# Decode trunk on one core: VectorE's sample steps moved ahead of its projection work, the mLSTM gate exponents in two row halves, the last norm's spread on ScalarE

## The chip, the cores and the metric

One core of a Trainium2 chip. The metric is the device time of one execution in microseconds (us); 3 runs of the kernel before have a median of 925.68 us, from 924.83 to 926.03.

## The reference, cut to what matters

One layer of a decoder over 512 prompt tokens and 32 sample tokens (8 sequences of 4, each with 2048 past positions in a paged cache), all in float32.

```python
z = x @ w_in + b_in                               # 27 feature tiles of 128
qk = silu(causal_dwconv(m_qk, width 4))           # mLSTM queries and keys
h = mlstm_chunkwise(q, k, v, ig, log_sigmoid(f))  # weights exp(b_t - b_s + i_s - m_t), causal
o_c, o_s, o_w = nsa_attend(...)                   # compressed, top-16 selected, window keys
mix = [sigmoid(o) * head_norm(h), g0*o_c + g1*o_s + g2*o_w]
x1 = layer_norm(ALPHA*x + mix @ w_out)
y  = layer_norm(ALPHA*x1 + (gelu(conv(u_a)) * conv(u_b)) @ w_down)   # u = x1 @ w_up
```

For the samples, attention over the past needs the keys of 16 pages of each of the 8 sequences transposed, scored, and the values of the same pages read once more. The mLSTM weights of a chunk come as one exponent per pair of tokens: the input gate less the running sum of the forget gates of one token, less the running maximum of the other.

## The kernel before, in words

Features stand on partitions, the 544 tokens on columns. The large products (projection, output, up, down) are made of tiles: the function `project` (L1867) runs 8 steps of k, each with 6 matmuls (a weight split in a high and a low part, against high and low parts of the input, each on 256 and on 288 columns). ScalarE makes the high part of a weight piece (`split_hi`, L500, which waits until the tile two before has ended), VectorE the low part (`split_lo`, L508), each two tiles ahead. A tile writes one of two PSUM pairs, so tile n+2 waits (`evicted`, L2100) until the result of tile n has been taken out: by VectorE (`rows_out`) for tiles 1 to 10 and 23 to 26, by ScalarE for the gates (0), the eight mLSTM query and key tiles 11 to 18 (`conv_rows`, followed by VectorE's `rows_conv`, L1148, four operations of 568 columns) and the sigmoid tiles 19 to 22 (`sigmoid_rows`, L808).

The samples' attention is woven into the projection tiles 5 to 26. Its order is written out by hand: `decode_halves` (L138) yields halves (g, i, h), with g the group of four sequences, i the beat (four of window keys from -4, then one for each four pages of a quad), h the half of a beat; `halves_of_tiles` (L188) gives each a tile and the step k of that tile after which TensorE runs it. Tiles 5 to 20 take five halves each, after steps 0, 2, 3, 5 and 7; tiles 21 to 26 take four, after 0, 2, 4 and 6. TensorE transposes keys, scores them, compresses them, and for the group before transposes probabilities and sums values. A half belongs to all engines. ScalarE runs the copies, exponentials and so on of the halves of tile n+1 in its turn n: the first of them right behind `split_hi`, then tile n's own result, the second, `silu`, and then the others. VectorE runs the halves of tile n in its turn n, all of them before `split_lo` of tile n+2 and before the results of tile n (L1367), so behind the results of tile n-1. Its steps: the eviction of scores (`past_scores`, L1268), the selection of the 16 best blocks (`select`, L1299), the probabilities of the selection (`selected_probs`, L1317) and of the window (`window_probs`, L1263). Transposed keys and probabilities and scores share PSUM banks 5 and 6 in turn (`next_bank`, L1896): a bank is free when what it held two turns before has been taken out.

Pages come by DMA into a ring of 8 slots. Two queues issue them: SP the even pages of a beat, POOL the odd ones (`stream_keys` and `stream_values`, L540 and L572). Both take the halves in order; a key page of beat i+2 waits for the slot that TensorE frees in beat i. SP's queue carries the weights too. POOL, behind its last issue, sets up the mLSTM exponents.

Then comes a stage of prompt attention (32 pairs of scores, softmax, transposes, values) with the four mLSTM chunks woven in. In each chunk TensorE makes the gate exponents (`exponents`, L2251) as a product over 40 rows: `gl` (L237) holds the gate differences in rows 0 to 7 and ones in rows 32 to 39, `rows` (L297) holds a unit pattern against the first and the negated running maxima against the second (POOL, `masked_rows`, L724). Two matmuls of 512 columns, one for each half of the heads, write banks 2 and 3; VectorE takes them out in `decay` (L1451). The output, up and down products follow. The last norm ends the kernel: token sums on TensorE, variance on VectorE, root on ScalarE, reciprocal and a diagonal matrix on VectorE (`inverse`, L1738), a product with ones that spreads it (`spread`, L2412), multiplication out of PSUM on VectorE, scale and bias on ScalarE (L1127), and the store.

Of the kernel before, what the change touches and what calls it, by code (L numbers as in the profile page):

```python
# [18 lines left out]
ALU = mybir.AluOpType  # L19
# [168 lines left out]
def halves_of_tiles():  # L188

    body = [x for x in decode_halves() if x[0] < GROUPS]  # L190
    tail = [x for x in decode_halves() if x[0] >= GROUPS]
    out = [[] for _ in range(ZT)]
    for n, x in enumerate(body):
        t = len(body) // (TAIL - FIRST)
        out[FIRST + n // t].append(((0, 2, 3, 5, 7)[n % t], x))
    for n, x in enumerate(tail):
        out[TAIL + n // 4].append(((0, 2, 4, 6)[n % 4], x))
    return out


# [3 lines left out]
def layer(nc, a):  # L204
    with ExitStack() as ctx:
# [28 lines left out]
        gfx = sb("gfx", [64, NT])  # L234
        gf = gfx[0:8, :]
        dsc = sb("dsc", [128, 1256])
        gl = sb("gl", [40, NT])  # L237
        gi = gl[0:8, :]
        ga = sb("ga", [8, NT])
        gmx = sb("gmx", [40, T])  # L240
# [53 lines left out]
        comb = smem[:, 3072:3592].rearrange("p (q t e) -> p q t e", q=2, t=4)  # L294
        sq = smem[:, 3592:4104].rearrange("p (h d) -> p h d", h=H)
        carried = zt[:, Z_G, 0:520].rearrange("p (s t e) -> p s t e", s=2, t=4)
        rows = mixt[0:40, 0:4, :].rearrange("p k c -> p (k c)")[:, 0:2048].rearrange("p (s c) -> p s c", s=2)  # L297
        hc = zt[:, Z_MV:Z_MV + 4, :].rearrange("p k c -> p (k c)")[:, 0:2048].rearrange("p (j h d) -> p j h d", j=4, h=H)
        wv = zt[:, Z_SV:Z_CV + 1, :].rearrange("p k c -> p (k c)")[:, 0:2080].rearrange("p (i h c) -> p i h c", i=4, h=H)

# [396 lines left out]
        @block.gpsimd  # L697
        def _(pool):

            pool.memset(uq[:, :, 0:3], 0.0).then_inc(prep, 1)  # L700
            pool.memset(ga[:, 0:T], 1.0).then_inc(prep, 1)
            pool.memset(gl[:, :], 0.0).then_inc(gl_set, 1)
            pool.wait_ge(gl_set, 1)
            pool.memset(gl[32:40, :], 1.0).then_inc(gl_set, 1)
            pool.wait_ge(gl_set, 2)
            pool.memset(qb, 0.0).then_inc(nd_z, 1)
            issued = [0]
            pool.wait_ge(xin[KD // 2 - 1], 16)
            for i in range(-SG, 0):
                stream_keys(pool, mybir.EngineType.Pool, 1, 0, i)  # L710
                issued[0] += 1
            pool.wait_ge(consts, NCONST)
            for n in range(ZT):
                for _, (g, i, h) in HALVES[n]:
                    stream(pool, mybir.EngineType.Pool, 1, issued, g, i, h)
            pool.wait_ge(nd_s, SETS * GROUPS)
            pool.memset(rows, 0.0).then_inc(gl_set, 1)
            pool.wait_ge(gl_set, 3)
            for s in range(2):
                pool.tensor_copy(by_block(rows[0:8, s]).rearrange("p (q t) c -> p q t c", q=2),  # L720
                                 bc(by_head(ident[0:8, 0:8]), 128)).then_inc(ml_rc, 1)
            pool.wait_ge(ml_rc, 2)

            def masked_rows(c):  # L724
                if c >= 2:
                    pool.wait_ge(ml_d, c - 1)
                    pool.wait_ge(ml_wv, c + 1)
                pool.tensor_tensor(by_block(rows[32:40, c % 2]).rearrange("p (q t) c -> p q t c", q=2),
                                   gm_neg[:, 128 * c:128 * c + 128].unsqueeze(1).unsqueeze(1).broadcast_to([8, 2, 4, 128]),
                                   bc(by_head(ident[32:40, 32:40]), 128), ALU.mult).then_inc(ml_r, 1)  # L730
                pool.wait_ge(ml_r, c + 1)

            for c in range(2):
                masked_rows(c)
            pool.wait_ge(w_used, ZT)
            pool.memset(tv[:, :, :, HD:HD + 1], 1.0).then_inc(prep, 1)
            pool.memset(scp, 0.0).then_inc(np_z, 1)
            pool.wait_ge(g_em, 1)
            pool.wait_ge(prep, 3)
            pool.wait_ge(tok_k_ev, 2 * (QT + 1))  # L740
            pool.wait_ge(stored, 16 * 3)
            for i in range(QT):
                pool.wait_ge(tok_v_ev, i + 1)
                pool.tensor_tensor(wv[:, i, :, :], tv[:, i, :, :], bc(emp[:, 64 + 8 * i:72 + 8 * i], HD + 1),
                                   ALU.mult).then_inc(ml_wv, 1)
                if i >= 2:
                    masked_rows(i)

            pool.wait_ge(np_pv, PAIRS)
            pool.memset(qm, 0.0).then_inc(sd_qz, 1)  # L750

            pool.wait_ge(sd_sc, 2)
            pool.wait_ge(sd_in, 48)
            pool.wait_ge(sd_int, 2)
            for t in range(4):
                c3 = ctv[:, t, :].rearrange("p (b e) -> p b e", b=NB)
                pool.tensor_tensor(c3, c3, bc(scb[:, 8 * t:8 * t + 8], HD), ALU.mult).then_inc(sd_cm, 1)
            pool.wait_ge(sd_end, 2)
            pool.wait_ge(hist, 16)
            pool.memset(uf[:, :, 0:2], 0.0).then_inc(prep, 1)  # L760
            for n in range(UP):
                pool.wait_ge(f_u, n + 1)
                pool.tensor_copy(fc[:, n, 0:2], uf[:, n % 4, 512:514])  # L763
                pool.tensor_copy(fc[:, n, 2:18].rearrange("p (b t) -> p b t", b=NB),
                                 by_sequence(uf, n, 6)[:, :, 4:6]).then_inc(f_last, 1)

        @block.scalar
        def _(act):
# [353 lines left out]
            act.activation(mean[:, T:NT], q4[2][:, 1, HALF:HALF + NS], ACT.Copy).then_inc(ln_act, 1)  # L1122
            act.activation(s4[:, 0:1], epsc[:, :], ACT.Sqrt)
            root(1)
            for m in range(KD):
                act.wait_ge(ln_u, m + 1)
                act.activation(xt[:, m, :], xt[:, m, :], ACT.Identity, bias=vec("ln2_b", m),  # L1127
                               scale=vec("ln2_w", m)).then_inc(ln_y, 1)

        @block.vector  # L1130
        def _(dve):
# [232 lines left out]
                    to_mix(p - 1)  # L1364

            for n in range(ZT):
                for _, half in HALVES[n]:  # L1367
                    decode_half(*half)
                if n == 4:
                    rows_out(n)  # L1370
# [14 lines left out]
                    table_rows()  # L1385
                if n == 3:
                    gate_columns()

            def token_columns(i):
                dve.wait_ge(tok_t, 3 * i + 1)  # L1390
# [347 lines left out]
            def inverse(n):  # L1738

                dve.wait_ge(ln_act, act_stat(n, "root"))  # L1740
                link(dve.reciprocal(tok5[:, :], tok5[:, :]))
                dg = scaled[0]
                dve.tensor_tensor(by_block(dg[:, 0:T]), ident.unsqueeze(1).broadcast_to([128, 4, 128]),
# [113 lines left out]
            for m in range(3, KD):  # L1857
                last = centred(m)
            link(last)
            dve.wait_ge(ln_pe, pe_stat(1, "spread"))  # L1860
            for m in range(KD):
                dve.tensor_tensor(xt[:, m, 0:T], xt[:, m, 0:T], bank[6], ALU.mult)
                dve.tensor_tensor(xt[:, m, T:NT], xt[:, m, T:NT], bank[7][:, 0:NS], ALU.mult).then_inc(ln_u, 1)

        @block.tensor
        def _(pe):
# [384 lines left out]
            def exponents(c):  # L2251
# [5 lines left out]
                    pe.wait_ge(tok_v_ev, QT + 1)  # L2257
                    pe.wait_ge(tok_k_ev, 2 * QT + 2)
                for q in range(2):
                    mm = pe.matmul(bank[2 + q], gl[:, token_rows(c)], rows[:, c % 2, 512 * q:512 * q + 512],  # L2260
                                   start=True, stop=True)
                mm.then_inc(ml_d, 1)

            def states(c):
# [145 lines left out]
                token_means(norm_rows[0][2], bank[7]).then_inc(ln_pe, 1)  # L2410

            def spread(n):  # L2412
                pe.wait_ge(ln_dve, 2 * n + 2)
                pe.matmul(bank[6], ones, scaled[0][:, 0:T], start=True, stop=True)
                pe.matmul(bank[7][:, 0:NS], ones, scaled[0][:, T:NT], start=True, stop=True).then_inc(ln_pe, 1)

# [172 lines left out]
```

## Time and profile before

| | us |
|---|---|
| median of 3 runs | 925.68 |
| profiled execution, its own time | 931.38 |
| its span, first to last instruction | 929.4 |
| TensorE busy | 865.3 (93%) |
| VectorE busy | 594.2 (64%) |
| ScalarE busy | 406.0 (44%) |
| GpSimd busy | 134.6 (14%) |
| mean granted TensorE clock | 0.938 of full |

All times of rows are from the start of the span. Busy times of TensorE are of pipelined matmuls: an engine that is 100% busy at a granted clock of 0.50 does half the work. Projection with the samples' attention lies at 0 to 289 us, prompt attention with the mLSTM at 289 to 440, output and up products to about 780, down and the last norm behind it.

### The profile page before, as it was taken

To read this page: it belongs to the slowest core of one execution; us is meant where nothing else is said; L and a number is where in the kernel's file an instruction comes from. 1 tells how busy PE (TensorE), PEld (TensorE's weight loads), DVE (VectorE), ACT (ScalarE), POOL (GpSimd) and SP (SyncE) were. 2 spreads that over 40 slices of the span, in tenths; PEclk is the share of its full clock that TensorE was granted. 3 is DMA by queue.
4 is the path that set the end of the run, shared out by engine and by line. 5 is a ranking of instruction groups with operands and counts; after the bars stand their busy time and mean duration, and the time that the engine had idled before them with its cause. 6 is when DMAs were issued, how large, how long until landed. Compare 5 with 4: busy or idle time off the path is not lost.

```text
span 929.4 us, 20070 instructions
## 1 busy us (share of the span) xinstructions
PE 865.3 (93%) x7843; PEld 784.5 (84%) x7843; DVE 594.2 (64%) x1227; ACT 406.0 (44%) x769; POOL 134.6 (14%) x248
## 2 busy tenths in 40 slices
PE   6999989898988899897889999999999999999994
PEld 6998878777877666665769999999999999999993
DVE  4622336541433687877887678888888888755556
ACT  4332345543523233477233355655555556222213
POOL 2022213253432200000010011111111111000000
PEclk9999989899989577999689999999999999999997
DMA  9267686677566000000214245222222222223212
GB/s 325 71 214 241 228 282 216 211 229 229 154 213 227 2 1 1 1 1 8 98 47 130 89 159 181 92 92 81 80 92 91 92 85 73 91 80 94 87 58 96
DMA packets 54888, 112.46 MB, mean 121 GB/s; under 512 B 7089, under 2 KB 32466, under 8 KB 54282
## 3 DMA queue, kind: packets, MB, share of 16 engines
q1 hardware_dynamic: 47074, 90.54, 29.7%
q0 software_dynamic: 6528, 17.83, 6.2%
q10 hardware_dynamic: 1192, 2.81, 0.8%
q8 instruction: 62, 1.02, 0.4%
q14 instruction: 32, 0.26, 0.1%
HBM read 105.54 MB, written 12.40 MB: 127 GB/s over the span
## 4 chain that ended last, share of the span: by engine, by line
PE 80%; DVE 10%; issue 4%; DMA 2%; ACT 2%; POOLq 2%; POOL 0%; ACTq 0%; SPq 0%; DVEq 0%
PE q L1883 32%; PE q L1881 29%; PE q L2204 2%; PE q L2220 2%; PE q L2230 2%; PE q L1945 1%; POOLq L517 1%; DVE xt L1428 1%; PE q L1933 1%; DMA arena<-in_pool 1%; PE q L2294 1%; DVE xt L1441 1%; PE q L1999 1%; PE q L1956 1%; PE q L2194 1%
## 5 line engine op out<-in xcount | busy, mean ns | idle before, releaser
L498 DVE TENSOR_TENSOR wring_r<-wring,whi_r 128x1024 fp32r<-128x1024 f32 (+1 forms) x101 | 120.2, 1191 | 162.3 <-ACT whi_r L495 162.0
L1881 PE MATMUL q<-arena_r,whi_r 128*128 128x256 f32 x712 | 212.4, 298 | 11.9 <-DVE wring_r L498 8.9
L1883 PE MATMUL q<-arena_r,whi_r 128*128 128x288 f32 (+1 forms) x712 | 214.1, 301 | 0.0
L1883 PE MATMUL q<-arena_r,wring_r 128*128 128x288 f32 (+1 forms) x712 | 213.7, 300 | 0.0
L1881 PE MATMUL q<-arena_r,wring_r 128*128 128x256 f32 x712 | 202.8, 285 | 0.0
L495 ACT ACTIVATE whi_r<-wring 128x1024 fp32r<-128x1024 f32 (+1 forms) x101 | 104.4, 1035 | 212.9 <-PE q L1883 212.5
L1883 PE MATMUL q<-xt_r,whi_r 128*128 128x290 f32 (+1 forms) x552 | 166.1, 301 | 0.0
L1881 PEld LDWEIGHTS q<-arena_r,whi_r 128*128 128x128 f32 x712 | 137.4, 193 | 23.4 <-DVE wring_r L498 8.9
L1881 PE MATMUL q<-xt_r,whi_r 128*128 128x256 f32 x552 | 157.0, 284 | 0.0
L1881 PEld LDWEIGHTS q<-arena_r,wring_r 128*128 128x128 f32 x712 | 137.5, 193 | 0.0
L1883 PEld LDWEIGHTS q<-arena_r,whi_r 128*128 128x128 f32 x712 | 137.5, 193 | 0.1
L1883 PEld LDWEIGHTS q<-arena_r,wring_r 128*128 128x128 f32 x712 | 137.2, 193 | 0.0
L1881 PEld LDWEIGHTS q<-xt_r,whi_r 128*128 128x128 f32 x552 | 106.4, 193 | 0.0
L1883 PEld LDWEIGHTS q<-xt_r,whi_r 128*128 128x128 f32 x552 | 106.1, 192 | 0.0
L987 ACT ACTIVATE whi<-q 128x128 f32<-128x128 f32 (+3 forms) x64 | 24.9, 436 | 67.3 <-PE q L2230 67.2
L553 POOL DMA_DIRECT2D arena<-in_pool x64 | 34.7, 542 | 132.3 <-PE q L1945 66.1
L826 ACT ACTIVATE mixt<-q 128x512 f32<-128x512 f32 x40 | 23.9, 598 | 68.0 <-PE q L1933 56.9
L1883 PE MATMUL q<-zt_r,whi_r 128*128 128x288 f32 x176 | 51.9, 297 | 0.0
L1881 PE MATMUL q<-zt_r,whi_r 128*128 128x256 f32 x176 | 49.0, 280 | 0.0
L763 POOL COPY smem<-zt 128x2 f32<-128x2 f32 x42 | 8.8, 211 | 247.1 <-ACT zt L1097 247.1
L581 POOL DMA_DIRECT2D arena<-in_pool x64 | 34.4, 537 | 53.8 <-issue 25.1
L1096 ACT ACTIVATE zt<-cst,sm 128x512 f32<-128x512 f32 x42 | 30.5, 727 | 26.5 <-DVE cst L1800 26.5
(458 smaller groups left out, 1564.0 us busy)
## 6 DMA issues: line engine op xcount, KB each, us to landing
wring<-in_w_up SPq DMA_DIRECT2D x42, 512.0 KB, 3.4
wring<-in_w_in SPq DMA_DIRECT2D x27, 512.0 KB, 5.0
arena<-in_pool SPq DMA_DIRECT2D x64, 192.0 KB, 3.5
arena<-in_pool POOLq DMA_DIRECT2D x64, 192.0 KB, 4.3
wring<-in_w_down SPq DMA_DIRECT2D x24, 448.0 KB, 3.2
arena<-in_pool SPq DMA_DIRECT2D x64, 64.0 KB, 2.2
arena<-in_pool POOLq DMA_DIRECT2D x64, 64.0 KB, 2.6
wring<-in_w_out SPq DMA_DIRECT2D x8, 512.0 KB, 7.1
```

Of the source, the lines that this page charges most:

```text
L495: return eng.activation(out, src, ACT.Copy)
L498: return eng.tensor_tensor(out, src, hi.bitcast(F32), ALU.subtract)
L553: eng.dma_start(pages[:, o % PAGE_RING, :], rows[k][:, 0:384]).then_inc(pg_land[o % PAGE_RING], 16)
L581: eng.dma_start(home[:, s, :], rows[s][:, 384:512]).then_inc(land, 16)
L826: act.activation(skt[i % SG], t, ACT.Copy).then_inc(nd_te, 1)
L987: act.activation(ptb[:, m % 2, g, 0:w], bank[4 + g][:, 0:w], ACT.Copy).then_inc(np_te, 1)
L1096: act.activation(u[:, 2:514], t[:, 0:T], ACT.Identity, bias=b, scale=-1.0)
L1881: pe.matmul(out[:, 0, 0:HALF], w, x[:, 0:HALF], start=(kk == 0 and n == 0), stop=(end and n == 2))
L1883: mm = pe.matmul(out[:, 1, 0:width - HALF], w, x[:, HALF:width], start=(kk == 0 and n == 0), stop=(end and n == 2))
L2204: return pe.matmul(bank[6][p, 128 * j:128 * j + 128], v, probs, start=start, stop=stop, skip_group_check=True)
L2220: mm = pe.matmul(bank[g][:, 0:w], q_of(GQ * g + j, i), zt[64 * g:64 * g + 64, (Z_SK, Z_WK)[k], 0:w], start=True, stop=True)
L2230: mm = pe.transpose(bank[4 + g][:, 128 * kk:128 * kk + 128], pb[:, m % 3, g, 128 * kk:128 * kk + 128], ident)
```

## The change

Three parts. (1) VectorE's turn n in the projection runs the halves of tile n+1, as ScalarE's does: those after steps 0 to 2 at once, ahead of `split_lo` of tile n+2 and of the results of tile n, the others behind these. The 23 halves of tiles 21 to 26 get new places. (2) The gate exponents' second half of heads gets its own copy of its 40 rows, in rows 64 to 103 of `gl` and `rows`; each of the two matmuls reads its own rows. POOL's set-up is cut in two accordingly, with one more copy of 8 rows by 512. (3) In the last norm ScalarE makes the diagonal matrix in five operations and copies the spread product to SBUF in two; VectorE then multiplies each of the 8 tiles in one operation of 544 columns instead of two out of PSUM.

```diff
@@ def halves_of_tiles():
-    for n, x in enumerate(tail):
-        out[TAIL + n // 4].append(((0, 2, 4, 6)[n % 4], x))
+    places = [(0, 1, 3, 5, 7), (0, 2, 4, 7), (4, 6), (0, 1, 3, 5, 7), (0, 2, 4, 6), (0, 2, 4)]
+    order = iter(tail)
+    for n, at in enumerate(places):
+        out[TAIL + n] = [(k, next(order)) for k in at]
...
-        gl = sb("gl", [40, NT])
+        gl = sb("gl", [104, NT])
...
-        rows = mixt[0:40, 0:4, :].rearrange("p k c -> p (k c)")[:, 0:2048].rearrange("p (s c) -> p s c", s=2)
+        rows = mixt[0:104, 0:4, :].rearrange("p k c -> p (k c)")[:, 0:1024].rearrange("p (s c) -> p s c", s=2)
...
@@ def _(pool):
             for s in range(2):
-                pool.tensor_copy(by_block(rows[0:8, s]).rearrange("p (q t) c -> p q t c", q=2),
-                                 bc(by_head(ident[0:8, 0:8]), 128)).then_inc(ml_rc, 1)
-            pool.wait_ge(ml_rc, 2)
+                for q in range(2):
+                    pool.tensor_copy(by_block(rows[64 * q:64 * q + 8, s]),
+                                     bc(by_head(ident[0:8, 0:8])[:, q], 128)).then_inc(ml_rc, 1)
+            pool.wait_ge(g_rdy, 1)
+            pool.tensor_copy(gl[64:72, 0:T], gi[:, 0:T]).then_inc(ml_rc, 1)
+            pool.wait_ge(ml_rc, 5)
...
-                pool.tensor_tensor(by_block(rows[32:40, c % 2]).rearrange("p (q t) c -> p q t c", q=2),
-                                   gm_neg[:, 128 * c:128 * c + 128].unsqueeze(1).unsqueeze(1).broadcast_to([8, 2, 4, 128]),
-                                   bc(by_head(ident[32:40, 32:40]), 128), ALU.mult).then_inc(ml_r, 1)
+                for q in range(2):
+                    last = pool.tensor_tensor(by_block(rows[64 * q + 32:64 * q + 40, c % 2]),
+                                              gm_neg[:, 128 * c:128 * c + 128].unsqueeze(1).broadcast_to([8, 4, 128]),
+                                              bc(by_head(ident[32:40, 32:40])[:, q], 128), ALU.mult)
+                last.then_inc(ml_r, 1)
...
@@ def _(act):
             root(1)
+            act.wait_ge(ln_dve, 4)
+            dg = scaled[0]
+            for c in range(QT):
+                act.activation(dg[:, 128 * c:128 * c + 128], ident, ACT.Copy, scale=tok5[:, c:c + 1])
+            act.activation(dg[:, T:NT], ident[:, 128 - NS:128], ACT.Copy, scale=tok5[:, 4:5]).then_inc(ln_act, 1)
+            act.wait_ge(ln_pe, pe_stat(1, "spread"))
+            act.activation(rstd[:, 0:T], bank[6], ACT.Copy)
+            act.activation(rstd[:, T:NT], bank[7][:, 0:NS], ACT.Copy).then_inc(ln_act, 1)
...
@@ def _(dve):
             for n in range(ZT):
-                for _, half in HALVES[n]:
+                steps = HALVES[n + 1] if n + 1 < ZT else []
+                soon = [half for at, half in steps if at <= 2]
+                for half in soon:
                     decode_half(*half)
...
                 if n == 3:
                     gate_columns()
+                for _, half in steps[len(soon):]:
+                    decode_half(*half)
...
                 dve.wait_ge(ln_act, act_stat(n, "root"))
+                if n == 1:
+                    dve.reciprocal(tok5[:, :], tok5[:, :]).then_inc(ln_dve, 1)
+                    return
...
-            dve.wait_ge(ln_pe, pe_stat(1, "spread"))
+            dve.wait_ge(ln_act, 8)
             for m in range(KD):
-                dve.tensor_tensor(xt[:, m, 0:T], xt[:, m, 0:T], bank[6], ALU.mult)
-                dve.tensor_tensor(xt[:, m, T:NT], xt[:, m, T:NT], bank[7][:, 0:NS], ALU.mult).then_inc(ln_u, 1)
+                dve.tensor_tensor(xt[:, m, :], xt[:, m, :], rstd, ALU.mult).then_inc(ln_u, 1)
...
@@ def exponents(c):
                 for q in range(2):
-                    mm = pe.matmul(bank[2 + q], gl[:, token_rows(c)], rows[:, c % 2, 512 * q:512 * q + 512],
-                                   start=True, stop=True)
+                    p = slice(64 * q, 64 * q + 40)
+                    mm = pe.matmul(bank[2 + q], gl[p, token_rows(c)], rows[p, c % 2, :], start=True, stop=True)
...
@@ def spread(n):
-                pe.wait_ge(ln_dve, 2 * n + 2)
+                if n == 0:
+                    pe.wait_ge(ln_dve, 2)
+                else:
+                    pe.wait_ge(ln_act, 7)
```

## Rows read from the trace of the kernel before

**Rows 1.** The page, the chain that ended last, share by engine.

```profile
PE 80%; DVE 10%; issue 4%; DMA 2%; ACT 2%; POOLq 2%; POOL 0%; ACTq 0%; SPq 0%; DVEq 0%
```

**Rows 2.** TensorE's waits: line waited for, us in total, times, longest.

```profile
PE q L1964 <- DVE smem L1275: 4.3, 1, 4.3
PE q L2270 <- DVE smem L1453: 4.2, 1, 4.2
PE q L2033 <- DVE smem L1322: 4.0, 1, 4.0
...
PE q L1925 <- DVE smem L1278: 3.4, 1, 3.4
...
PE q L1933 <- DMA arena<-in_pool: 2.6, 3, 1.5
...
PE q L1995 <- DVE arena L1266: 2.2, 1, 2.2
```

**Rows 3.** Stretches: length, busy us (instructions) of each engine; TensorE's clock, DMA, GB/s.

```profile
560.00:900.00 340.00, 340.00 (x2685) 339.72 (x2684) 256.99 (x413) 159.09 (x258) 33.02 (x76) 1.00 0.28 92
...
130.26:135.00 4.74, 4.74 (x22) 4.74 (x23) 0.00 (x0) 0.61 (x2) 0.55 (x1) 0.50 0.96 392
168.42:173.00 4.58, 4.58 (x20) 4.39 (x20) 0.00 (x0) 3.45 (x4) 0.00 (x0) 0.50 0.10 40
...
259.58:265.20 5.62, 5.62 (x36) 4.95 (x37) 3.21 (x7) 1.66 (x2) 0.09 (x1) 0.50 0.51 195
309.20:337.00 27.80, 27.74 (x163) 20.61 (x165) 16.89 (x68) 8.20 (x33) 1.90 (x1) 0.50 0.00 1
337.80:357.40 19.60, 17.24 (x167) 12.82 (x165) 18.47 (x57) 8.87 (x32) 0.00 (x0) 1.00 0.01 2
```

**Rows 4.** Timeline of VectorE, 128.5 to 130.5: start, us, engine, line.

```profile
129.39 0.61 DVE L1275 TENSOR_SCALAR smem<-q,arena 128x384 f32<-128x384 f32 x1
```

**Rows 5.** Timeline of ScalarE and of VectorE, 155 to 168.

```profile
155.46 0.20 ACT L868 ACTIVATE zt<-q 128x32 f32<-128x32 f32 x1 [2.00 <-PE q L2020]
...
163.30 0.19 DVE L1302 MAX8 dsc<-zt 128x8 f32<-128x32 f32 x1
...
167.62 0.75 DVE L1275 TENSOR_SCALAR smem<-q,arena 128x512 f32<-128x512 f32 x1
```

**Rows 6.** Timeline of POOL's queue: key pages of beats 5, 9 and 15.

```profile
162.08 1.15 POOL L553 DMA_DIRECT2D arena<-in_pool  x2 [1.07 <-issue]
...
182.15 1.14 POOL L553 DMA_DIRECT2D arena<-in_pool  x2 [3.04 <-PE q L1945]
...
221.64 1.15 POOL L553 DMA_DIRECT2D arena<-in_pool  x2 [1.08 <-PE q L1945]
```

**Rows 7.** DMA issues, 150 to 170: count, KB, median us to landing.

```profile
arena<-in_pool POOLq DMA_DIRECT2D x7, 192.0 KB, 4.9
```

**Rows 8.** Timeline of ScalarE, 249 to 259.

```profile
250.91 1.28 ACT L813 ACT_TABLE_LOAD   x1
...
256.49 2.03 ACT L873 ACTIVATE smem<-smem,sm 128x2080 f32<-128x2080 f32 x1 [2.12 <-DVE sm L1315]
```

**Rows 9.** Timeline of TensorE: exponents of chunks 1 and 2, a pair of prompt scores.

```profile
324.75 3.69 PE L2260 MATMUL q<-mixt,gl 40*128 40x512 f32 x4
...
342.36 1.88 PE L2260 MATMUL q<-mixt,gl 40*128 40x512 f32 x4
...
426.54 1.13 PE L2220 MATMUL q<-zt 64*128 64x512 f32 x4
```

**Rows 10.** Timeline of VectorE and GpSimd, 304 to 308.

```profile
304.22 3.16 DVE L1441 TENSOR_SCALAR xt<-xt,gcol 128x128 f32<-128x128 f32 x2
```

**Rows 11.** Timelines: ScalarE at 125.9; TensorE and ScalarE in the last norm.

```profile
125.88 0.30 ACT L805 ACTIVATE mixt<-q,col 128x32 f32<-128x32 f32 x1
...
916.91 1.71 PE L2414 MATMUL q<-cst 128*128 128x512 f32 x2 [2.21 <-DVE cst L1745]
...
920.89 5.98 ACT L1127 ACTIVATE xt<-xt,col 128x544 f32<-128x544 f32 x8 [5.25 <-DVE xt L1863]
```

More of the change, by code:

```diff
@@ L703, in _ @@
             pool.wait_ge(gl_set, 1)
-            pool.memset(gl[32:40, :], 1.0).then_inc(gl_set, 1)
+            pool.memset(gl[32:40, :], 1.0)
+            pool.memset(gl[96:104, :], 1.0).then_inc(gl_set, 1)
             pool.wait_ge(gl_set, 2)
```

## The prediction

> **What bounds the kernel now.** I read the chain that ended last, then TensorE's waits, then the stretches in which it ran, then what stood ahead of each releaser on its engine. The chain is 80% TensorE [rows 1]: a microsecond counts only where TensorE idles, or works at half clock. From 560 to 900 us it never idles and takes 340/2685 = 0.127 us a matmul, so a step k (6 matmuls) is 0.76 us and a bare tile 6.1 us [rows 3]. Its long waits are before 320 us. In the projection four are for VectorE's sample steps: 3.4 us (L1925 for `past_scores`), 4.3 (L1964 for `past_scores`), 2.2 (L1995 for `window_probs`), 4.0 (L2033 for `selected_probs`), and 2.6 us in three waits are for key pages [rows 2]. Each long wait is paid twice: behind it the granted clock is 0.50 of full, that is 1.2 in place of 2.4 GHz, though TensorE is busy throughout: 4.7 us from 130.3, 4.6 from 168.4, 5.6 from 259.6 [rows 3]. At full clock these would take half, so they cost 2.4, 2.3 and 2.8 us.
>
> **Part 1, VectorE's order.** The instructions are the same. Only those steps move that belong after steps 0 to 2: they no longer stand behind `split_lo` and the results of the tile before, these now stand behind them. No DMA moves on SP or POOL but with TensorE's slots and the tail's new places.
>
> First wait: the scores' eviction started at 129.4 [rows 4], behind `rows_conv`, though TensorE had made them by about 124.1. In the new order it is over by 125, before TensorE asks (126.9). Gain 3.4 + 2.4 = 5.8. `rows_conv` waits for ScalarE's result in either order and ends no later.
>
> Second wait: `select` began at 163.3, eviction at 167.6, while the importance that `select` needs was copied at 155.5 [rows 5]. `select` takes 167.6 - 163.3 = 4.3 us; it can now run from 155.7 to 160.0, the eviction at 162, and TensorE passes at 164.1. Behind it `split_lo` and `rows_conv` end 3 to 4 us later than before, at 167; the next tile starts at about 168.6, so their cover is thin but there. What is late next: the pages of beat 5. POOL issues them at 162.1 in two pieces [rows 6], the second at 162.7; such pages land 4.9 us after issue [rows 7], at 167.5; TensorE would want them at 166.7. Gain 4.3 + 2.3 - 0.8 = 5.8.
>
> Third wait: 2.2 us go, but I book nothing. From the pages of beat 9 on, POOL issues without rest: from 182.2 to 221.6 its queue goes through six beats, 6.6 us each [rows 6], against some 5 us that TensorE needs for a beat without waits. TensorE already waits for the last pages (the 2.6 us). What it gains behind 181 us it waits for them again. Bounds: 0 and the whole 2.2 plus 1.7 of half clock. I take 0, as POOL's start follows from TensorE's own slot at 181.4, whose shift is counted above.
>
> Fourth wait, in the tail: `select` stood behind `split_lo`, and the window for exponential and probabilities was one half beat. With the new places importance comes two steps (1.5 us) earlier, `select` runs from about 247.7 to 252.1, and the probabilities are wanted only in tile 24. But on ScalarE the exponential (2.03 us) is now tile 23's first half, so it stands **ahead** of the sigmoid rows of tile 22, for which tile 24 waits. Both table loads, 1.28 each, are paid as before [rows 8], only the order is turned. From tile 22's end at 250.0: `split_hi` 1.06, load 1.28, exponential and its sum 2.2, load 1.28, sigmoid 0.9 = 256.8. TensorE wants the bank one bare tile later, 250.0 + 6.1 = 256.1. New wait 0.7 to 0.8, shorter than any behind which the rows show half clock. Gain 4.0 + 2.8 - 0.8 = 6.0.
>
> Part 1 together: 5.8 + 5.8 + 0 + 6.0 = 17.6 us.
>
> **Part 2, two row halves.** Per chunk, 4 instructions of 512 columns on 40 rows take 3.69 us at half and 1.88 at full clock. The same form for the prompt scores, whose two halves lie on rows 0 to 63 and 64 to 127, takes 1.13 at full clock [rows 9]. By that row the halves run side by side: 0.75 us saved at full clock, 1.5 at half. Chunks 1 and 3 run at half clock with TensorE always busy (from 309 to 337 for chunk 1 [rows 3]): 1.4 each after overlap. In chunk 0 TensorE waits 4.2 us for VectorE right behind [rows 2], in chunk 2 VectorE is busy for 18.5 of 19.6 us [rows 3]: both 0. Sum 2.8, bounds 0 and 4.5. The Trainium skill ("TensorEngine Tiling (Array Packing)", Theoretical Speedup) gives up to 2 times for 64 rows or less; by it a chunk at half clock would save 1.8, the sum be 3.6.
>
> POOL's two products of 1024 become four of 512, plus a copy of 512: some 0.2 us more for each masked row set. The set-ups of chunks 0 and 1 lie in POOL's slack before 289. That for chunk 2 lies where VectorE's two small operations took 3.16 us instead of 0.6 [rows 10], because GpSimd ran. Either VectorE slips in between the shorter pieces (up to 1 us gained before `decay`) or all is 0.2 later: I take 0. The Trainium skill ("SBUF — State Buffer", SBUF: two separate sides) has it that VectorE and GpSimd share a port pair, held for a whole instruction; the row agrees, and by it the shorter pieces would give the 1 us.
>
> **Part 3, the last norm.** VectorE's two operations for the diagonal ended at 916.86. ScalarE's five: 0.30 us at 32 columns with an operand per partition, 5.98/8 = 0.75 at 544 [rows 11], so 0.38 at 128, less some 0.11 of overlap: 4 x 0.27 + 0.30 = 1.4, ending at 917.5. The product then runs wholly at half clock (+0.1), and two copies (0.70) stand before VectorE's first multiplication, where it used to be held by its centring until 920.07. 917.5 + 2.2 + 0.7 + 0.1 for handing over = 920.5. VectorE's single operation (0.73) saves 0.1. From there ScalarE's 0.75 us a tile is the bound in either version, so VectorE's shorter steps bring nothing. Cost 0.3 to 0.4; bounds -0.3 and +0.8; I take 0.4 slower.
>
> **Sum.** 17.6 + 2.8 - 0.4 = 20.0 us. It is made in the profiled execution, whose 931.38 us lie 5.7 above the median; waits like these recur in every run, so I take it from the median: 925.7 - 20.0 = 905.7.
>
> **Rivals.** (a) POOL's issue already binds at the second wait: for beats 5 to 7 TensorE waits for pages, and of that gain of 5.8 us only 0.8 is left. For: at 162.1 POOL issues back to back; against: before beat 9 it waits 3.0 us for TensorE again [rows 6]. 905.7 + 5.0 = 910.7. 0.12. (b) ScalarE's turned order costs the fourth gain: exponential waits longer for `select`, sigmoid after it, and the clock falls again: 905.7 + 5 = 910.7 as well, seen at another place. 0.10. (c) The row halves do not run side by side: 908.5. 0.07. (d) POOL's pace is no bound, the third wait's 3.9 us and VectorE's 1 come too: 900.8. 0.10. (e) Slower: the mLSTM stage changes clock. From 309 to 337 us the clock stays at half although TensorE is 100% busy, from 337.8 to 357.4 it is full [rows 3]. Nothing in the rows says what lets it rise. If the two full stretches (this and one from 373 to 389, together 29.7 us of busy TensorE) and some of what follows stayed at half, less the 5 us of idle in them, that costs about 25: 930.5. It decides once over 20 us of busy time turn half. Against: shorter exponents take little work out. 0.04. The forecast itself: 0.57.
>
> **How the numbers follow.** 905.7 is the likeliest. The clock of stages not touched may shift by 3 us either way. Down to (d) less 2, up to (a) or (b) plus 4: 899 to 915. About 0.2% (1.9 us) is what a measurement of this kernel can tell from no change. Faster by over that: every case but (e), since (a), (b) and (c) together still give 905.7 + 5 + 5 + 2.8 = 918.5: 0.93; within it, by (e) in part, 0.03; slower 0.04.
>
> **What would show it.** Right: the waits of L1925, L1964, L1995 and L2033 for VectorE gone or under 1 us; clock 1.00 from 124 to some 180; page waits of L1933 and L1999 grown to 5 us or more in the last beats of group 1; a new wait for ScalarE's sigmoid at a tile's start near 240; exponents at about 1.1 us (full) or 2.2 (half); first L1127 no earlier behind the last projection matmul than before. Wrong: a wait for `split_lo` at a tile's start in the projection, or a full-clock stretch lost behind 290.

## The result, and the profile after

The change took the kernel from 925.63 us (924.6 to 927.37, 7 runs) to **917.46 us** (910.9 to 919.92, 7 runs): a ratio of 0.9899, 95% interval 0.9865 to 0.9933. That is a gain of 8.2 us by the medians (9.3 by the ratio) where 20.0 were forecast. The profiled execution took 919.92 us, with a span of 917.8 against 929.4; 11.6 us apart, because before's profiled run lay 5.7 us above its median and after's 2.5.

TensorE's waits after the change (us in total, times, longest), to be held against [rows 2]:

```profile
PE q L2292 <- DVE smem L1473: 7.7, 4, 3.6
PE q L2021 <- DMA arena<-in_pool: 6.7, 4, 3.6
PE q L1955 <- DMA arena<-in_pool: 6.1, 6, 2.1
PE q L2439 <- ACT cst L1137: 2.9, 1, 2.9
PE q L2191 <- DVE arena L1412: 2.5, 1, 2.5
PE q L1903 <- ACT zt L823: 0.2, 1, 0.2
```

The four waits for VectorE's sample steps, 13.9 us, are gone. In their place stand waits for DMA: for key pages (L1955, formerly L1933) 6.1 us in place of 2.6, and for value pages (L2021, formerly L1999) 6.7. The wait for the decay (L2292, formerly L2270) went from one of 4.2 to four of 7.7 together. The sigmoid wait, forecast at 0.8, is 0.2.

**Where the gain is lost** shows when one follows the same instruction through both traces. After the first removed wait the changed kernel is 4.8 us ahead (137.81 against 142.64 us at the first score set of group 1), although it had been 1.2 us behind at 123: that wait brought its 5.8 and a little more. At beat 7 it is 7.5 ahead, where 10.4 were forecast (5.8 twice, less that 1.2): the second wait brought 2.7. At tile 21 it is 7.7: the third brought 0.2. At the first prompt scores it is 9.1 (281.61 against 290.69): the fourth brought 1.4 of its 6.0. At the end it is 11.6. So two places take it, the second wait and the tail.

The second removed wait: TensorE on its timeline, with the stretch behind it (the third number from its end is the granted clock), then GpSimd's queue, then its page issues from 150 to 164 us with their median from issue to landing.

```profile
163.00 0.44 PE L1955 MATMUL q<-cst,arena 128*128 128x128 f32 x2 [1.66 <-DMA arena<-in_pool]
164.19 0.33 PE L1955 MATMUL q<-cst,arena 128*128 128x128 f32 x1 [0.75 <-DMA arena<-in_pool]
164.00:168.60 4.60, 4.41 (x49) 4.12 (x50) 2.70 (x9) 0.81 (x2) 1.08 (x2) 0.63 0.51 157
```
```profile
150.73 1.15 POOL L555 DMA_DIRECT2D arena<-in_pool  x2 [1.08 <-issue]
153.86 2.33 POOL L583 DMA_DIRECT2D arena<-in_pool  x4 [1.98 <-issue]
157.26 1.15 POOL L555 DMA_DIRECT2D arena<-in_pool  x2 [1.07 <-issue]
```
```profile
arena<-in_pool POOLq DMA_DIRECT2D x6, 192.0 KB, 5.8
```

GpSimd issues the pages of beat 5 at 157.26, against 162.08 before [rows 6]: 4.8 us earlier, which is the first wait's gain and nothing of the second's, since the queue works without a rest from 144.2 us on (149.0 before). The pages of that stretch then take 5.8 us to land (median of six); the two of beat 5 took 5.7 and 6.3, where the prediction had 4.9 for each. That figure was the median of seven issues; the same two pages in the trace before, issued at 162.08 and about 162.65, took

```profile
arena<-in_pool POOLq DMA_DIRECT2D x1, 192.0 KB, 4.9
arena<-in_pool POOLq DMA_DIRECT2D x1, 192.0 KB, 5.9
```

so about 1 us of the lateness could be read there. TensorE waits 2.4 us for them, and the clock is lower behind them (0.63 of full from 164.0 to 168.6).

The tail. SP's queue and ScalarE's before:

```profile
250.03 5.95 SPq L581 DMA_DIRECT2D arena<-in_pool  x8
256.50 0.75 ACTq L944 DMA_DIRECT2D relrow<-relone  x1
```

The same after, with TensorE's wait, and the queues' shares from 247 to 257 us (q10 is ScalarE's):

```profile
242.37 6.80 SPq L583 DMA_DIRECT2D arena<-in_pool  x8
244.24 0.75 ACTq L952 DMA_DIRECT2D relrow<-relone  x1
256.66 1.08 PE L2021 MATMUL q<-arena,cst 128*32 128x128 f32 x16 [3.58 <-DMA arena<-in_pool]
257.00:260.00 3.00, 3.00 (x27) 2.62 (x20) 0.00 (x0) 0.60 (x1) 1.46 (x3) 0.50 0.63 232
```
```profile
q10 hardware_dynamic: 608, 1.56, 39.8%
arena<-in_pool SPq DMA_DIRECT2D x8, 64.0 KB, 5.4
arena<-in_pool POOLq DMA_DIRECT2D x4, 64.0 KB, 4.8
```

ScalarE's broadcast to relrow (2560 KB: a small table in device memory written out 128 times for each head) was issued at 256.50 before, behind the eight value transfers that TensorE wanted next (SP had issued them by 255.98). Its place in the program is unchanged, but ScalarE no longer waits for the selection, and it is now issued at 244.24, among these transfers. TensorE waits 3.6 us for them, and half clock follows.

The last norm on ScalarE, and the exponents by group (busy us, mean ns):

```profile
903.87 1.28 ACT L1136 ACTIVATE cst<-cst,sm 128x128 f32<-128x128 f32 x4 [0.43 <-DVE sm L1762]
905.41 2.08 PE L2439 MATMUL q<-cst 128*128 128x512 f32 x2 [2.91 <-ACT cst L1137]
909.34 5.96 ACT L1143 ACTIVATE xt<-xt,col 128x544 f32<-128x544 f32 x8 [0.86 <-DVE xt L1885]
L2283 PE MATMUL q<-mixt,gl 40*128 40x512 f32 x16 | 4.8, 676 | 0.6 <-DVE zt L1513 0.6
```

### The profile page after: what moved, and what is told of

It reads as the page before. It is cut to its first block, busy times and chain, and to the rows that moved or that the text cites. A ratio compares the mean times of both kernels' runs of the same rounds, so it can differ in the third digit from the quotient of the medians.

```text
span 917.8 us, 20077 instructions
## 1 busy us (share of the span) xinstructions
PE 852.0 (93%) x7843; PEld 775.1 (84%) x7843; DVE 593.0 (65%) x1217; ACT 409.6 (45%) x778; POOL 136.3 (15%) x256
## 4 chain that ended last, share of the span: by engine, by line
PE 78%; DVE 9%; DMA 5%; issue 3%; SPq 2%; ACT 2%; POOLq 1%; POOL 0%; ACTq 0%; DVEq 0%
PE q L1905 32%; PE q L1903 29%; DMA arena<-in_pool 4%; PE q L1967 2%; PE q L2242 2%; DVE xt L1448 2%; PE q L2226 2%; PE q L1955 1%; PE q L2252 1%; DVE xt L1461 1%; SPq L583 1%; PE q L2316 1%; PE q L2021 1%; SPq L519 1%; PE q L1978 1%
```

## The experiments

The theory after the first profile: part 1 removed what it was meant to remove, and about half of it was taken back by two transfers' paths, the issue of pages by SP and GpSimd, and the broadcast in the tail. The rivals: parts 2 and 3 cost the rest; or the DMA engines themselves are full. All times are medians in us; before's was 925.0 to 926.7 beside them. The ratios differ from the ratio of the medians by up to 0.2%, so a difference between two rows is given both ways where that matters. The rows come from several chips. In the last column is the time of the first prompt scores in the profiled run (290.7 before).

| kernel | us | ratio to before, 95% interval | scores at |
|---|---|---|---|
| the change | 917.46 | 0.9899 (0.9865 to 0.9933) | 281.6 |
| the same, again (after_again) | 915.92 | 0.9888 (0.9857 to 0.9919) | 277.2 |
| part 1 alone (p1_only) | 919.06 | 0.9913 (0.9884 to 0.9942) | 276.4 |
| part 2 alone (p2_only) | 924.21 | 0.9975 (0.9950 to 1.0001) | 289.5 |
| part 3 alone (p3_only) | 926.21 | 1.0014 (0.9987 to 1.0040) | 288.5 |
| VectorE's order alone (order_only) | 916.08 | 0.9907 (0.9881 to 0.9933) | 276.7 |
| tail's places alone (places_only) | 926.91 | 1.0024 (1.0001 to 1.0047) | 289.4 |
| change, broadcast 2 tiles later (rel_late) | 919.16 | 0.9937 (0.9912 to 0.9962) | 271.9 |
| change, broadcast after tile 6 (rel_early) | 917.62 | 0.9916 (0.9896 to 0.9935) | 280.9 |
| change, broadcast in 8 pieces (rel_split) | 913.07 | 0.9855 (0.9815 to 0.9894) | 276.6 |
| change, 12 value sets from fixed pages (const_pages) | 908.34 | 0.9830 (0.9801 to 0.9858) | 270.5 |
| **change, page numbers kept (keep_ids)** | **899.54** | 0.9726 (0.9687 to 0.9765) | 263.1 |
| before, page numbers kept (before_keep) | 919.03 | 0.9931 (0.9905 to 0.9957) | 281.4 |
| order and rows, numbers kept (order_rows_keep) | 899.84 | 0.9712 (0.9682 to 0.9742) | 263.7 |
| change, kept and 8 pieces (keep_split) | 902.84 | 0.9739 (0.9700 to 0.9778) | 266.9 |
| the same, kept and 8 pieces (order_rows_keep_split) | 903.11 | 0.9760 (0.9723 to 0.9797) | 266.2 |

**The parts one by one.** Each applies its hunks of the change to the kernel before, and nothing else.

> Part 1 alone (VectorE's order and the tail's places; row halves and last norm as before). Theory A (the waits for VectorE went, but 8 of the 17.6 us were lost to waits for pages and for the tail's value transfers, and to half clock behind them): about 9 us faster than before, 916.6, with 2 us or more of page waits at the second removed wait and 3 to 4 us of waits for values of the second group in the tail. Theory B (part 1 gave what was forecast and parts 2 and 3 took it back): 908 to 910. Theory C (the row halves carry a good part of the gain): slower than 920.

> Part 2 alone (the spread of gate differences in two row halves). Forecast: 2.8 us faster than before, 922.8, exponents' four matmuls at 1.0 to 1.1 us at full clock against 1.88. Theory A (VectorE's decay is late next in every chunk): between 0 and 2 us faster, 924 to 925.6, with the wait for the decay longer by what the exponents are shorter. Theory B (GpSimd's smaller pieces hold VectorE up, or the clock of the stage falls): slower than 926.5.

> Part 3 alone (last norm's diagonal and copies on ScalarE). Forecast and theory A: 0.4 to 0.7 us slower than before, 926.0 to 926.3; from the end of the 20 small products to the first of ScalarE's eight scalings 6.6 to 6.9 us, against 6.2 before. Theory B (it saves, since VectorE's multiplications are shorter): 0.3 us faster or more. Theory C (it costs much more than its own stage shows): over 927.5.

Part 1 gains 7.1 us, part 2 1.9, part 3 changes nothing that can be measured (+0.1). Their sum of 8.9 is the change's 8.2 within the spread. So the shortfall lies in part 1; that parts 2 and 3 took it back is refuted. In part 2's profile the exponents' sixteen matmuls fall from 11.1 to 5.1 us:

```profile
L2267 PE MATMUL q<-mixt,gl 40*128 40x512 f32 x16 | 5.1, 718 | 0.0
322.65 2.02 PE L2267 MATMUL q<-mixt,gl 40*128 40x512 f32 x4
339.27 1.03 PE L2267 MATMUL q<-mixt,gl 40*128 40x512 f32 x4
PE q L2276 <- DVE smem L1459: 6.7, 4, 3.6
```

At half clock (2.02 against 3.69) and at full (1.03 against 1.88) the halves run side by side [rows 9], and the wait for the decay, over all four chunks, grows from 4.2 to 6.7 us in return. GpSimd's shorter pieces have an effect of their own, in chunk 0:

```profile
303.05 2.23 DVE L1447 TENSOR_SCALAR xt<-xt,gcol 128x128 f32<-128x128 f32 x2
```

These are the two small operations that took 3.16 us before [rows 10]. They stand ahead of `decay`, and the stretch from the start of the exponents to the product behind `decay` falls from 6.86 to 5.92 us. The four kernels with neither part 2 nor new places have 3.16 here, and p2_only, the change and its repetition 2.23.

**Order and places of part 1 apart.**

places_only has this hunk alone, order_only the two hunks of VectorE's loop alone.

```diff
-    for n, x in enumerate(tail):
-        out[TAIL + n // 4].append(((0, 2, 4, 6)[n % 4], x))
+    places = [(0, 1, 3, 5, 7), (0, 2, 4, 7), (4, 6), (0, 1, 3, 5, 7), (0, 2, 4, 6), (0, 2, 4)]
```

> VectorE's new order in the tiles alone, the tail's places as before, row halves and last norm as before. Theory A: 6 to 7.5 us faster than before (the gain that stood at tile 21 in the changed kernel was 7.7, and the tail's wait for selected probabilities of 4.0 us stays, or shrinks by the 4.3 us of the selection that no longer stand behind the split): 918 to 920. Theory B (order and places work only together): within 2 us of before.

> The tail's new places alone, VectorE's order as before, row halves and last norm as before. Theory A: the first three waits for VectorE stay (3.4, 4.3, 2.2 us); the fourth (4.0) goes, but a wait for values of 3 to 4 us takes its place, so 0 to 2.5 us faster than before, 923.5 to 926. Theory B (the places are what gains in the tail): 6 us faster, 920.

VectorE's order alone gives all of part 1 (8.9 us). The fourth wait, booked at 6.0 and put down to the places, falls from 4.0 to 1.9 by the order alone, with a wait for values of 1.9 behind it:

```profile
PE q L1937 <- DMA arena<-in_pool: 4.9, 6, 1.5
PE q L2003 <- DMA arena<-in_pool: 4.8, 4, 1.9
PE q L2037 <- DVE smem L1322: 1.9, 1, 1.9
```

The places remove the rest of it, but with them TensorE waits 2.5 us in place of 1.1 for VectorE's copy behind the first prompt scores (L2191 in the change), and they gain nothing on the whole.

**The broadcast.** rel_late and rel_early change one number, `if n == TAIL + 1:` to `TAIL + 3` and to `6`. rel_split issues it head by head:

```diff
-                if n == TAIL + 1:
-                    act.wait_ge(rel_out, 16)
-                    act.dma_start(relrow.ap(), relone.ap().unsqueeze(1).broadcast_to([H, 128, NREL])).then_inc(rel_out, 16)
+                if 6 <= n < 6 + H:
+                    act.wait_ge(rel_out, 16)
+                    act.dma_start(relrow.ap()[n - 6:n - 5], relone.ap()[n - 6:n - 5].unsqueeze(1)
+                                  .broadcast_to([1, 128, NREL])).then_inc(rel_out, 16)
```

> The changed kernel with ScalarE's 2.56 MB broadcast from relone to relrow issued two tiles later (after tile 24 instead of tile 22). Theory A (this transfer delays the value transfers of the second group in the tail, and that wait and the half clock behind it cost 3.6 + 1.5 us): the wait for values near 256 us under 1 us, time about 5 us below the changed kernel, 912. Theory B (the value transfers are late by their own issue, whatever else runs): the wait stays at 3 us or more, time as the changed kernel, 917. Theory C (the broadcast's end is late next, the reload of the table or the scores behind it wait): the wait near 256 us gone, and a new one of 3 us or more for the table behind 281 us, time 916 to 918.

> The changed kernel with ScalarE's 2.56 MB broadcast issued after tile 6 instead of tile 22. The run with it two tiles later reached the first prompt scores at 271.9 us in place of 281.6, but then waited 7.3 us for the table that is read back from it. Theory A (the broadcast delays the values in the tail, and late, the table): both waits gone, since it is long over; 5 to 9 us faster than the changed kernel, 908 to 913. Theory B (the 9.7 us of the late version came from something else, or the transfer costs the same among the pages of the first group): page waits of 3 us or more before 120 us, time as the changed kernel, 917.

> The changed kernel with the broadcast to relrow cut into eight pieces of 320 KB, one after each of the tiles 6 to 13. As one piece after tile 6 it took away the 3.6 us wait and the half clock in the tail (tail stage 5.1 us shorter), and cost 4.7 us of page waits between 72 and 91 us. Theory A (those waits came from the lump, which took the DMA engines for some 10 us): the pieces hide, page waits before 120 us under 1 us, 4 to 5 us below the changed kernel: 912 to 913.5. Theory B (the DMA engines are the bound in the first group as well, so that any 2.56 MB among the pages costs its time): the waits come back in small pieces, 916.5 to 918.

In rel_late no value wait is left behind 240 us, and the first prompt scores come at 271.9, 9.7 us earlier. Half of that was gained ahead of the tail, where nothing had been edited, so it is the spread between two profiles. The broadcast's price is in the stretch from the first selected probabilities to the prompt scores: 32.2 us in the change and 31.4 in its repetition, 27.0 in each of rel_late, rel_early and rel_split. But the third theory of its expectation came true: the table is read back from what the broadcast wrote, and the time is no better (919.2).

```profile
258.92 0.75 ACTq L952 DMA_DIRECT2D relrow<-relone  x1
271.91 0.49 PE L2242 MATMUL q<-zt 64*128 64x128 f32 x4 [1.21 <-DVE zt L1184]
281.12 5.38 PE L2191 MATMUL q<-cst,zt 128*128 128x128 f32 x24 [7.26 <-DVE arena L1412]
```

Issued early in one piece the broadcast brings these 5 us and gives them up at 72 to 91 us in four waits for the first pages (4.7 us). In eight pieces these shrink to 0.5 us, and the median is 913.1, 4.4 below the change; on another chip and with intervals that overlap, so the gain is not sure.

**The queues' pace.** const_pages takes fixed pages for values 4 to 15 of group 0 (that part of the computation is another one); keep_ids computes all of the reference and only remembers registers:

```diff
+            at = [first + step * k for k in range(n)]
+            if any((eng, x) not in KEPT for x in at):
...
+                for x, page in zip(at, ids):
+                    KEPT[eng, x] = page
-            return [a["pool"][bass.DynSlice(page, 1), :, :].rearrange("a p c -> (a p) c") for page in ids]
+            return [a["pool"][bass.DynSlice(KEPT[eng, x], 1), :, :].rearrange("a p c -> (a p) c") for x in at]
```

A queue loads pages of one parity for the keys, and of the same parity for the values, so each value number had been loaded before.

> The changed kernel, but the values 4 to 15 of the first group are read from fixed pages, so that SP and GpSimd load no page numbers for them (part of the computation is left out: these values come from other pages; the bytes moved are the same). Theory A (both queues need 6.6 us a beat from beat 9 on, 2 us of it for these four numbers, and TensorE is held to that): beats 9 to 14 in 4.6 to 5.2 us each, the waits for the last pages (6.1 + 6.7 us in the changed kernel) down by 5 us or more, time 5 to 8 us below the changed kernel. Theory B (the transfers themselves are slow, the DMA engines being 70 to 90% busy): the pace stays above 6 us, time within 1.5 us of the changed kernel.

> The changed kernel, but a queue that has loaded a page's number for its key half keeps it in the register and does not load it again for the value half. The reads from fixed pages gave 908.3. Theory A (the loads of numbers set the pace of both queues from beat 9 on): the same gain and more, since the values 0 to 3 and those of the second group are issued faster too: 905 to 909. Theory B (fixed pages gained by a lighter form of transfer, not by the loads): beats 9 to 14 still over 6 us each, 914 to 918.

Both point the same way: 9 and 18 us below the change by the medians, 6 and 16 by the ratios. GpSimd's queue in the change, and with kept numbers:

```profile
181.21 1.15 POOL L555 DMA_DIRECT2D arena<-in_pool  x2 [1.08 <-PE q L1967]
184.35 2.33 POOL L583 DMA_DIRECT2D arena<-in_pool  x4 [1.98 <-issue]
187.75 1.15 POOL L555 DMA_DIRECT2D arena<-in_pool  x2 [1.07 <-issue]
```
```profile
186.08 1.14 POOL L561 DMA_DIRECT2D arena<-in_pool  x2 [1.07 <-issue]
187.74 2.29 POOL L589 DMA_DIRECT2D arena<-in_pool  x4 [0.51 <-issue]
191.10 1.14 POOL L561 DMA_DIRECT2D arena<-in_pool  x2 [1.07 <-issue]
192.50 2.29 POOL L589 DMA_DIRECT2D arena<-in_pool  x4 [0.26 <-issue]
```

The first three lines are the change's. A beat takes 6.5 us of the queue in it, 3.1 of them in the gaps ahead of the issues; with four numbers kept the gap ahead of the values falls from 2.0 us to between 0.3 and 0.5, and the beat to 5.0, TensorE's own pace. SP's queue had the same pace (issues at 180.51, 187.12, 193.62 in the change). The Trainium skill ("Perfetto Trace Analysis", What "DMA-bound" means) has it that a kernel bound on the issuing sequencer shows that engine's track as solid DMA slices; here the slices fill 3.5 of 6.5 us, and the queue is the bound all the same, so the measurement decides. What the waits are then:

```profile
PE q L2298 <- DVE smem L1479: 3.4, 4, 1.9
PE q L2197 <- DVE arena L1418: 2.5, 1, 2.5
PE q L2027 <- DMA arena<-in_pool: 1.1, 2, 0.8
PE q L1961 <- DMA arena<-in_pool: 0.9, 2, 0.6
130.00:262.00 132.00, 130.56 (x1699) 112.42 (x1698) 59.08 (x147) 69.10 (x132) 59.58 (x104) 1.00 0.78 246
```

Of these 132 us TensorE is busy 130.6, and at full clock throughout. The DMA engines move more (246 GB/s) in them than in the change (234): they were not full, which settles the other rival. The tail's value wait is down to 0.8 too, with the broadcast where it was: SP issues 12 value transfers in 7.5 us where it needed 6.8 for 8.

**Both edits together, and each side of the change with kept numbers.**

> The changed kernel with both edits: page numbers kept, and the broadcast in eight pieces after tiles 6 to 13. Theory A (two separate bounds behind the removed waits for VectorE): their gains add, 9 + 4.5: 902 to 906, no wait over 1.5 us between 40 and 270 us. Theory B (one bound, the DMA engines' time): no more than the better of the two alone, 908.

> As the one with both edits, but with the tail's places and the last norm as in the kernel before (VectorE's order, row halves, kept numbers, broadcast in pieces). The tail's places alone made the kernel no faster (926.9 against 925.0). Theory A (they gained nothing only because the wait for values stood behind): with the values early the old places are slower again, by the wait for selected probabilities of 1.9 us and its half clock, less 0.6 us for the last norm: 1 to 3 us above the version with them. Theory B (the new places are worth nothing or cost in any case): as fast or 1 to 2 us faster.

> The kernel before, with page numbers kept in registers and nothing else changed. The changed kernel with them took 899.5. Theory A (the four waits for VectorE bind before, the queues only behind them): the queues have little to give here, the page waits of 2.6 us and some half clock behind them; 3 to 6 us faster than before, 920 to 923, so that the change is worth 20 us or more where the queues do not bind, as forecast. Theory B (the queues' pace of 6.6 us a beat binds before as well, and VectorE's waits hide behind it): 10 us or more faster than before, under 916, and the change is worth less than 16 us on top of it.

> VectorE's order, row halves and kept page numbers, with the tail's places and the last norm as before. Theory A (with the values issued faster the tail's new places are worth the wait for selected probabilities and its half clock, 1.9 + 1 us, less 0.6 us for the last norm): 901 to 903 against 899.5. Theory B (the places are worth nothing here too): 898 to 899.5.

> The changed kernel once more, unchanged, for a second profile. Theory A (its time varies with how late the page transfers land): page and value waits of another size than the 12.8 us of the first profile, and a time that moves with them, 911 to 920; the same places wait (second removed wait, last beats of the first group, tail's values). Theory B (waits are the same in every run, and the clock alone varies): the same waits within 0.5 us each.

The two edits do not add: 902.8, no better than kept numbers alone, since the tail's wait was gone already and the pieces bring 3.6 us of page waits. Places and last norm are worth nothing with the queues relieved either (899.84 and 903.11 without them, 899.54 and 902.84 with them). before_keep shows what the forecast was worth: its waits for VectorE are those of [rows 2],

```profile
PE q L1970 <- DVE smem L1281: 4.3, 1, 4.3
PE q L2039 <- DVE smem L1328: 4.0, 1, 4.0
PE q L1931 <- DVE smem L1284: 3.3, 1, 3.3
PE q L2001 <- DVE arena L1272: 2.2, 1, 2.2
```

and it runs 919.03 us. It gained 7.4 us by the medians and 6.4 by the ratio (interval 4.0 to 8.8), a little more than the 3 to 6 expected. In its profile 8.3 us lie between the second and the fourth wait, where before had 3.1 us of waits for pages and values and a lower clock behind them (230 to 240 us at 0.77, now 1.00). With kept numbers on both sides the change is worth 919.03 - 899.54 = 19.5 us (0.9726/0.9931 = 0.979, so 19, and some 4 us either way by the intervals). On one chip, without places and last norm, it is 919.03 - 899.84 = 19.2. The same change that gives 8 us where the queues bind gives some 19 where they don't.

That this is near the forecast's 20.0 is in part luck. Part 1's four waits, followed from the same instruction in before_keep to that in keep_ids, bring 5.2, 6.5, 2.4 and 4.3 us, where the prediction had 5.8, 5.8, 0 and 6.0: one term too low makes up for one too high.

after_again has the same waits in the same places, of other sizes: pages 6.9 us in 7, values 4.0 in 3, the one in the tail 2.97; the prompt scores come at 277.2 in place of 281.6. So these waits vary from run to run by microseconds.

## Why the prediction was wrong

**The mechanism of part 1 was right, and its prices as waits on VectorE too.** All four waits went (the fourth by half with the new order alone, the rest with the places), the sigmoid wait is 0.2 for 0.8, the third wait's gain was waited for again as said (the changed kernel is 11.1 us ahead at beat 10 and 7.4 at beat 13, behind waits for values), and the first gave its 5.8.

**The step that failed first is the second wait's "what is late next"**: "such pages land 4.9 us after issue, at 167.5; TensorE would want them at 166.7", priced at 0.8. The second page took 6.3 (5.9 already in the trace before), TensorE waited 2.4 us in two pieces, and the clock fell again behind them, for which the step had no price. Of 5.8 us 2.7 were left. With page numbers kept the same wait brought 6.5, so what took the rest is that its pages came late. This is rival (a) in all but its words: the queue had been issuing without rest since 149.0 us up to the pages at 162.1 [rows 6]. The prediction took "before beat 9 it waits for TensorE again" as evidence against, though that rest comes behind the pages in question.

**The second step that failed is the fourth wait's sum**, "gain 4.0 + 2.8 - 0.8 = 6.0". It looked for what ScalarE's turned order delays and not for what it brings forward. The broadcast stands behind that exponential in ScalarE's queue and moved 12.3 us earlier (256.50 to 244.24), while the values moved 7.7. Cost: 3.6 us of wait and about 1.5 of half clock; by rel_early 5.2 us together. That rival stood nowhere; (b) has its price, 5 us, but not its cause. The new places, on which the same sum rested, are worth nothing measurable.

**Rival (d), POOL's pace is no bound**, was rightly put low for this kernel: the third wait's gain was there at beat 10 and gone at beat 13. Taking the pace away shows what hid behind it: 16 to 18 us in the changed kernel, 6 to 7 in the one before.

**Part 2**: 2.8 forecast, 1.9 measured (interval from 4.6 to nothing); the stage from the prompt scores on is 3.7 us shorter in the change's profile and 4.6 in part 2's own, in part by the clock (chunk 3's exponents ran at full clock there and at half before). The prediction's "both 0" holds for chunk 2 (4.27 us from the exponents to the product behind `decay` became 4.15) and fails for chunk 0: 0.9 us came there, from VectorE's two operations beside GpSimd. The prediction had seen that term ("up to 1 us gained") and took 0. Chunk 1 gave 1.0 for the 1.4 forecast. **Part 3**: 0.4 slower forecast; from the end of the last small product to the first scaling 6.19 us became 6.84, so 0.65 slower in the profile; the runs (0.1 slower, interval from 1.2 faster to 3.7 slower) do not resolve it.

**Rival (e)**, a change of clock in the recurrent stage, was priced at 25 us and given 0.04. It exists at a smaller size: part 1 alone, with the same instructions as before in that stage, took 155.0 us for it in its profiled run against 150.2 before and 147.7 with VectorE's order alone. Windows of 15 us from the stage's middle, part 1 alone and then order alone:

```profile
336.42:351.42 15.00, 14.94 (x86) 12.32 (x85) 10.73 (x34) 4.22 (x15) 0.00 (x0) 0.55 0.01 2
351.42:366.42 15.00, 15.00 (x91) 9.48 (x89) 10.64 (x32) 5.41 (x18) 0.00 (x0) 0.54 0.00 1
```
```profile
336.73:351.73 15.00, 14.85 (x98) 10.73 (x97) 12.65 (x46) 5.04 (x20) 0.00 (x0) 0.77 0.01 2
351.73:366.73 15.00, 11.99 (x131) 8.80 (x132) 14.41 (x42) 7.31 (x24) 0.00 (x0) 1.00 0.00 1
```

Both kernels reach the prompt scores within 0.3 us of each other (276.4 and 276.7), and yet 7.3 us come between them in the stage, of which 1.4 are the longer wait for VectorE's copy. What decides the clock there is open, and one profile each does not say how often it happens; it may be a part of why the change's own seven runs spread over 9 us. The range (899 to 915) let the clock shift by 3 us and took no second failed term beside (a) or (b); both failed in part at once, and 917.5 lay outside.

## What to carry over

When a wait is removed, follow the queue that feeds the next one back to its last rest: only what the change shifts ahead of that rest shifts the transfers, so two gains in a row do not both arrive. A queue can be the bound with its slices far from solid: the gaps in which page numbers are loaded took nearly half of its time, and keeping the numbers in registers gave 16 to 18 us where the larger edit had given 8 to 9. A median time to landing is no price for one transfer: look up the very transfer in the trace before. And an engine made to run ahead brings its own transfers forward: look at what stands behind the moved instruction in its queue, the large DMAs first.

## What the hardware showed that was not expected

A page number loaded into a queue's register costs 0.4 to 0.5 us on GpSimd and SP alike, about as much as the issue of one transfer (0.58 and 0.43). The gap ahead of four issues is 1.98 us on GpSimd and some 2.15 on SP with the loads; without them it is 0.3 to 0.5 on GpSimd and can be as short as 0.25 on SP. Landing times are no constants: the same six 192 KB pages issued by GpSimd took a median of 5.3 us before (issued from 155.6 to 164.9 us), 5.8 in the change and 4.8 in its repetition, and 64 KB value transfers 2.0 to 2.4 us from 150 to 164 us, 4.8 to 5.4 beside the broadcast. Two small VectorE operations beside a GpSimd product took 3.16 us with the product in one piece of 1.89 us, and 2.23 with it in two pieces of 2.13 together. The recurrent stage took 144.6 to 155.0 us from the prompt scores on, over all kernels whose table loads were on time, at a mean granted clock of 0.78 to 0.89.
